# Layers 0, 1 and 3: the first block of the feed-forward part multiplies the input before its norm is known

## The reference, cut to what matters

```python
mod = (c_act @ ada_w[l] + ada_b[l])[:, None, :]
sh1, sc1, g1, sh2, sc2, g2 = jnp.split(mod, N_MOD, axis=-1)
...
x = x + g1 * token_mix(h, ...)
h = rmsnorm(x, norm2_g[l]) * (1.0 + sc2) + sh2
x = x + g2 * conv_ffn(h, ffn_up[l], conv_w[l], conv_b[l], ffn_down[l])

def conv_ffn(h, w_up, conv_w, conv_b, w_down):       # layers 0 and 1
    u = h @ w_up
    up = jnp.pad(u, ((0, 0), (pad, pad), (0, 0)))
    u = sum(up[:, i:i + S] * conv_w[i] for i in range(CONV_WIDTH)) + conv_b
    a, b = jnp.split(u, 2, axis=-1)
    return (jax.nn.gelu(a, approximate=False) * b) @ w_down

def sq_relu_mlp(h, w1, w2):                          # layers 2 and 3
    return jnp.square(jax.nn.relu(h @ w1)) @ w2
```

## Time and profile before

| | |
|---|---|
| median of 3 runs | 2072.24 us (2068.34 to 2072.96) |
| the profiled execution, its own time | 2072.03 us |
| its span, first to last instruction | 2070.3 us |
| PE busy | 2037.2 us, 98% |
| DVE busy | 1514.8 us, 73% |
| ACT busy | 987.7 us, 48% |
| POOL busy | 389.5 us, 19% |
| mean granted clock of TensorE | 0.994 of full speed |
| DMA | 396.38 MB, mean 191 GB/s |

### The profile page before, as it was taken

The page is one execution under the profiler, slowest core; times in us unless marked ns, Lnnn a source line. Parts: engine busy times, 40 slices in busy tenths (PEclk is TensorE's granted clock), DMA queues, the critical chain, the costliest instruction groups (busy, mean ns, idle before and its releaser), DMA issues.

```text
span 2070.3 us, 37115 instructions
## 1 busy us (share of the span) xinstructions
PE 2037.2 (98%) x14314; PEld 1872.9 (90%) x14314; DVE 1514.8 (73%) x2169; ACT 987.7 (48%) x1500; POOL 389.5 (19%) x284
## 2 busy tenths in 40 slices
PE   9999999999999999999999999999999999999998
PEld 8999999999999999999877888988888998899998
DVE  7877889977767999978988524898433285876554
ACT  4544456645445465553245533442143254755453
POOL 0421203300601213224101002120020021121120
PEclk9999999999999999999999999999999999999999
DMA  9775767786566656673554322366633244665553
GB/s 329 293 258 198 252 228 253 239 300 223 206 238 220 214 193 217 202 241 125 185 171 143 112 83 98 115 200 224 195 110 102 72 164 143 234 211 173 195 193 105
DMA packets 109739, 396.38 MB, mean 191 GB/s; under 512 B 12424, under 2 KB 13072, under 8 KB 109328
## 3 DMA queue, kind: packets, MB, share of 16 engines
q1 hardware_dynamic: 108304, 389.99, 55.7%
q0 software_dynamic: 1280, 4.20, 0.7%
HBM read 393.08 MB, written 1.05 MB: 190 GB/s over the span
## 4 chain that ended last, share of the span: by engine, by line
PE 79%; DVE 15%; DMA 2%; issue 2%; ACT 1%; POOL 0%; SPq 0%; DVEq 0%; ACTq 0%; POOLq 0%
PE bank L510 19%; PE bank L511 19%; PE bank L512 19%; DVE w_lo L1499 7%; DVE stage L1520 3%; DMA stage<-in_stream 2%; PE bank L708 2%; PE bank L635 2%; PE bank L634 2%; PE bank L633 2%; PE bank L711 2%; DVE conv L1790 1%; DVE conv L1795 1%; DVE rstd L1517 1%; PE bank L534 1%
## 5 line engine op out<-in xcount | busy, mean ns | idle before, releaser
L1499 DVE TENSOR_TENSOR w_lo<-stage,w_hi 128x1024 fp32r<-128x1024 f32 x536 | 716.7, 1352 | 411.0 <-ACT w_hi L1068 409.5
L1068 ACT ACTIVATE w_hi<-stage 128x1024 fp32r<-128x1024 f32 x536 | 566.3, 1060 | 840.3 <-PE bank L512 503.8
L510 PE MATMUL bank<-h_hi,w_hi 128*128 128x256 f32 (+1 forms) x2368 | 721.6, 305 | 8.6 <-DVE w_lo L1499 8.1
L511 PE MATMUL bank<-h_lo,w_hi 128*128 128x256 f32 (+1 forms) x2368 | 716.6, 303 | 0.0
L512 PE MATMUL bank<-h_hi,w_lo 128*128 128x256 f32 (+1 forms) x2368 | 716.4, 303 | 0.0
L510 PEld LDWEIGHTS bank<-h_hi,w_hi 128*128 128x128 f32 x2368 | 445.4, 188 | 37.4 <-DVE w_lo L1499 11.0
L512 PEld LDWEIGHTS bank<-h_hi,w_lo 128*128 128x128 f32 x2368 | 445.3, 188 | 21.5
L511 PEld LDWEIGHTS bank<-h_lo,w_hi 128*128 128x128 f32 x2368 | 445.5, 188 | 21.0
L1520 DVE SCALAR_TENSOR_TENSOR stage<-stage,cvec 128x1024 f32<-128x1024 f32 x192 | 259.9, 1355 | 12.5 <-DMA cols<-in_cols 9.2
L510 PE MATMUL bank<-f_hi,w_hi 128*128 128x256 f32 (+1 forms) x448 | 145.3, 324 | 0.0
L511 PE MATMUL bank<-f_lo,w_hi 128*128 128x256 f32 (+1 forms) x448 | 145.3, 324 | 0.0
(11 more groups left out here) (268 smaller groups left out, 3525.3 us busy)
## 6 DMA issues: line engine op xcount, KB each, us to landing
stage<-in_stream SPq DMA_DIRECT2D x728, 512.0 KB, 4.4
bias<-in_bias POOLq DMA_DIRECT2D x16, 256.0 KB, 3.4
cvec<-in_cvec SPq DMA_DIRECT2D x3, 512.0 KB, 5.1
X<-in_x SPq DMA_DIRECT2D x2, 512.0 KB, 6.1
decay<-in_decay SPq DMA_DIRECT2D x1, 1024.0 KB, 5.5
X<-in_x SPq DMA_DIRECT2D x1, 1024.0 KB, 8.5
out<-X SPq DMA_DIRECT2D x4, 256.0 KB, 2.1
rope<-in_rope SPq DMA_DIRECT2D x2, 256.0 KB, 4.7
```

The costliest lines, as they stand in the source:

```text
L510: mm(out, w_hi[:, slot, w], xh[:, c, 0:T], start=first, stop=False)
L511: mm(out, w_hi[:, slot, w], xl[:, c, 0:T], start=False, stop=False)
L1068: A(w_hi[:, m % NR, :], stage[:, n % NS, :], ACT.Copy).then_inc(hi_ready, 1)
L1499: do(V.tensor_tensor(w_lo[:, m % NR, :], stage[:, n % NS, :], w_hi[:, m % NR, :].bitcast(F32), ALU.subtract), unit_done, done_value(n))
```

## The change

For layers 0, 1 and 3:

- Block up0 (f0) multiplies raw_hi and raw_lo, the split of X*MUL without the norm. Each has two more columns, S and S+1, that hold the shift sh2, so a bank's column S is sh2 @ W. The products have 258 columns instead of 256. ScalarE makes raw_hi (raw_highs) and VectorE raw_lo (raw_lows), in two halves of 4 chunks behind the residual.
- TensorE makes the norm's sums before the third unit of up0 instead of before its first. The fill products and the chunkwise first unit are gone there. The blocks from up1 (f1) on use h as before.
- When rstd is there, VectorE copies column S (shifted) and multiplies each bank of up0 by rstd into tt (scale_first); ScalarE adds the shift in tt. The convolution (or relu) of block 0 then works on tt.
- The places of the weight splits move: three copies stand between ScalarE's squares and its root, and four splits on VectorE before the reciprocal. Block 0's elementwise work comes after up1's splits.
- In SCHEDULE the modulation of layer 1 starts at up2 instead of up0; for layer 2 it is every 3 units instead of 4 from ar1, and every 7 instead of 6 from up3.
- The first vector of layer 2's modulation for j < 4 takes one pass of 1024 with a scratch tile of its own (products).

```diff
-    (0, "k0", 0, 2, [(0, j) for j in range(4, 12)]), (0, "up0", 1, 3, [(1, j) for j in range(4)]),
-    (0, "dn0", 4, 1, [(1, 4), (1, 5)]), (1, "in", 5, 2, [(1, j) for j in range(6, 12)]),
-    (1, "ar1", 0, 4, [(2, 0), (2, 1)]), (1, "up3", 0, 6, [(2, 2)]), (1, "dn0", 0, 3, [(2, 3)]),
+    (0, "k0", 0, 2, [(0, j) for j in range(4, 12)]), (0, "up2", 0, 3, [(1, 0), (1, 1), (1, 2)]),
+    (0, "dn0", 2, 2, [(1, 3)]), (0, "dn0", 10, 1, [(1, 4), (1, 5)]), (1, "in", 5, 2, [(1, j) for j in range(6, 12)]),
+    (1, "ar1", 0, 3, [(2, 0), (2, 1)]), (1, "up3", 0, 7, [(2, 2)]), (1, "dn0", 0, 3, [(2, 3)]),
...
-                norm_sums(L, "n2")
-                fill_gap(L, "up0", 16)
-                feature_block(L, "up0", hh, hl, S, h_ready(L, "n2"), after_norm=(L, "n2"))
+                feature_block(L, "up0", raw_hi[L], raw_lo[L], S + 2, raw_ready(L), before={2: lambda: norm_sums(L, "n2")})
                 for b in range(1, FC // 2):
-                    feature_block(L, f"up{b}", hh, hl, S, nothing)
+                    feature_block(L, f"up{b}", hh, hl, S, h_ready(L, "n2") if b == 1 else nothing)
...
+            def late_norm(layer, ready, n):
+
+                advance(n - 4)
+                root_table(layer, "n2")
+                raw_highs(layer, ready, range(DC // 2))
+                advance(1)
+                squares(layer, "n2", ready, range(DC // 2), table=False)
+                advance(1)
+                raw_highs(layer, ready, range(DC // 2, DC))
+                advance(1)
+                squares(layer, "n2", ready, range(DC // 2, DC))
+                advance(3)
+                root(layer, "n2")
+                highs(layer, "n2", behind=(3,))
+
+            def shift_scaled(layer, g, n):
+
+                wait_taken(act, g)
+                A(tt[:, n, S:T2], tt[:, n, S:T2], ACT.Identity, bias=shifted[:, n:n + 1]).then_inc(s["scaled_ready"], 1)
+                act.wait_ge(s["scaled_ready"], 4 * layer + n + 1)
...
-                if vecs == 2:
+                if layer == 2 and j < 4:
+                    settle()
+                    do(V.scalar_tensor_tensor(products[:, :], w, 1.0, cvec[:, 0, :], ALU.mult, ALU.mult,
+                                              accum_out=MOD[:, par, 0, q:q + 1]))
+                elif vecs == 2:
...
+            def late_norm(layer):
+
+                advance(3)
+                norm(layer, "n2", behind=(4,))
+
+            def scale_first(layer, name):
+
+                for n in range(4):
+                    g = grp(layer, name, n)
+                    wait_filled(dve, g)
+                    do(V.tensor_scalar(shifted[:, n:n + 1], bank_of(g)[:, S:S + 1], 1.0, None, ALU.mult))
+                    settle()
+                    take(V.tensor_tensor(tt[:, n, S:T2], bank_of(g)[:, 0:S], rstd[:, 0:S], ALU.mult), g)
...
-                    ahead = 2 if nb == 0 else -2
+                    ahead = 1 if nb == 0 else -1
...
-                norm(L, "n2")
-                advance(1)
+                late_norm(L)
                 for b in range(FC // 2):
-                    g0 = most_of(L, f"up{b}")
+                    if b:
+                        g0 = most_of(L, f"up{b}", 2 if b == 1 else 0)
+                    else:
+                        advance(2)
+                        scale_first(L, "up0")
+                        advance(1)
```

More of the change, by code:

```diff
@@ L1038, in _ @@
                                         hooks={(0, 2, 0): lambda: norm_sums(2, "c2")})
-                        else:
-                            feature_block(L, f"f{b}", h_hi[L], h_lo[L], T, h_ready(L, "n2") if b == 0 else nothing,
-                                          after_norm=None if b else (L, "n2"))
+                        elif L == 3 and b == 0:
+                            feature_block(L, "f0", raw_hi[L], raw_lo[L], S + 2, raw_ready(L),
+                                          before={2: lambda: norm_sums(L, "n2")})
+                        else:
+                            feature_block(L, f"f{b}", h_hi[L], h_lo[L], T, h_ready(L, "n2") if (L, b) == (3, 1) else nothing)
                     base = 32 * (L - 2) + 16 * half
@@ L1090, in each, with root_table, squares @@
                     advance(1)
-            def squares(layer, name, ready, chunks):
+            def root_table(layer, name):
+                nth = NORMS.index((layer, name))
+                A(idle[0:1, nth:nth + 1], ones[0:1, 0:1], ACT.Sqrt).then_inc(s["idle"], 1)
+            def squares(layer, name, ready, chunks, table=True):
                 nth = NORMS.index((layer, name))
                 tok = tokens_of(name)
-                if 0 in chunks:
-                    A(idle[0:1, nth:nth + 1], ones[0:1, 0:1], ACT.Sqrt).then_inc(s["idle"], 1)
+                if 0 in chunks and table:
+                    root_table(layer, name)
                 for c in chunks:
@@ L1136, in norm, with raw_highs @@
                     highs(layer, name)
+            def raw_highs(layer, ready, chunks):
+                if 0 in chunks:
+                    ready(0)
+                    A(raw_hi[layer][:, :, S:S + 2], MOD[:, layer % 2, 0, 3 * DC:4 * DC].rearrange("p (c t) -> p c t", t=1).to_broadcast([P, DC, 2]),
+                      ACT.Copy).then_inc(s["raw_hi"], 1)
+                for c in chunks:
+                    ready(c)
+                    A(raw_hi[layer][:, c, 0:S], X[:, 0, c, :], ACT.Copy,
+                      scale=MUL[:, layer % 2, 0, 1, c:c + 1]).then_inc(s["raw_hi"], 1)
+            def late_norm(layer, ready, n):
[15 more added lines that the diff above has]
+                act.wait_ge(s["scaled_ready"], 4 * layer + n + 1)
             def first_norm(ready):
@@ L1443, in _ @@
                     for b in range(4 * half, 4 * half + 4):
-                        for part in range(2):
+                        late = L == 3 and b == 0
+                        if late:
+                            advance(2)
+                        else:
+                            for part in range(2):
+                                if (L, b) != (3, 1):
+                                    advance(1)
+                                if b % 4:
+                                    hidden2_hi(b - 1, part)
                             advance(1)
-                            if b % 4:
-                                hidden2_hi(b - 1, part)
-                        advance(1)
                         for n in range(4):
@@ L1606, in norm, with raw_lows @@
                 rest(layer, name, DC - 1)
+            def raw_lows(layer, chunks):
+                base = RAW_BEFORE[layer]
+                if 0 in chunks:
+                    dve.wait_ge(s["raw_hi"], base + 1)
+                    do(V.tensor_tensor(raw_lo[layer][:, :, S:S + 2],
+                                       MOD[:, layer % 2, 0, 3 * DC:4 * DC].rearrange("p (c t) -> p c t", t=1).to_broadcast([P, DC, 2]),
+                                       raw_hi[layer][:, :, S:S + 2].bitcast(F32), ALU.subtract), s["raw_lo"], base + 1)
+                for c in chunks:
+                    dve.wait_ge(s["raw_hi"], base + c + 2)
+                    do(V.scalar_tensor_tensor(raw_lo[layer][:, c, 0:S], X[:, 0, c, :], MUL[:, layer % 2, 0, 1, c:c + 1],
+                                              raw_hi[layer][:, c, 0:S].bitcast(F32), ALU.mult, ALU.subtract),
+                       s["raw_lo"], base + c + 2)
+            def late_norm(layer):
[8 more added lines that the diff above has]
+                    take(V.tensor_tensor(tt[:, n, S:T2], bank_of(g)[:, 0:S], rstd[:, 0:S], ALU.mult), g)
             def final_norm(layer):
@@ L1675, in residual @@
                                                 X[:, 0, c, :], ALU.mult, ALU.add), g0 + n)
+                if layer != 2 and name[:2] == "wo":
+                    settle()
+                    raw_lows(layer, range(4 * nb, 4 * nb + 4))
                 if before_norm:
```

92 lines of the change are left out of this document (68 added, 24 removed).

## The result

The change makes the kernel slower: 2076.44 us median of 20 runs against 2071.63 of 20 runs of before, a ratio of 1.0024 (+5.0 us), 95% interval 1.0016 to 1.0031, or +3.3 to +6.4 us. One run of before took 2725.8 us and is not in the ratio, which compares the fast runs of both kernels. The forecast was 2068.5, -3.5 us against its base. The side was wrong; the time lies in the stated range and near rival B.

A forecast was written before the change was run, and what follows sets the result against it. TensorE, busy 98%, was taken as the bound, with VectorE's weight splits feeding it. Terms +1.4 - 2.4 - 2.0 - 2.5 = -5.5 us, plus 2 for disturbances, gave -3.5 from 2072.0: 2068.5 us, range 2059 to 2078.

The forecast's parts named there:

- rival B: Slower: VectorE backlog at up2 in layers 0 and 1, GpSimd collisions, half clock, no modulation gain; +5, 2077 us; chance 0.22.
- the modulation's -2.5: Layer 2's modulation made in layer 1, with one pass and new spread: -2.5 us, bounds -5 to +3.
- Steps 1 and 3: Layer 0 from the output block to the norm's sums: ScalarE and VectorE feed in time, sums end at 287.5 without stall.
- Step 2: Start of up0: TensorE begins at once at 279.75 and runs units 0 and 1 to 285.2 free of a stall.
- the sign that its mechanism is wrong: New TensorE waits inside up0 itself would show the forecast wrong in its mechanism; no size given.
- Step 4: Up1 in layer 0: three weight copies delay the root, so TensorE stalls 2.1 us, then 0.5 us.
- Steps 5 and 6: Up2 in layer 0: late splits stall TensorE 2.6 us at the third unit, 3.7 at the fourth; up2 ends at 324.0.
- Layer 0's +1.4: Layer 0: 10.2 us of gap replaced by 2.2 of sums and 9.4 of stalls, +1.4 us.
- Layer 1's -2.4: Layer 1: stalls of 2.0, 0.4, 2.0 and 2.6 us, up3 at 42.6 instead of effectively 45.0 after the output product: -2.4 us.
- Layer 3's -2.0: Layer 3: stalls of 1.6 and 0.4 us at f1, which ends 25.9 instead of 27.9 us after the output product: -2.0 us.
- Disturbances, +2: Layers 0 and 1: splits meeting GpSimd products and half clock after waits add 2 us together, between nothing and 5.6.
- Two columns more: First-block products of 258 columns instead of 256 on 3 x 96 products: 0.25 us.

The follow-up runs named there:

- e1: The kernel before with the late norm in layer 3 only, SCHEDULE and two-pass modulation as before: ratio 0.9986, -2.9 us against before.
- e3: The kernel before with only the one pass of 1024 in place of two of 512, SCHEDULE as before: ratio 0.9955, -9.3 us against before.
- e7: The kernel before with the one pass and the late norm in layer 3 only, SCHEDULE as before: ratio 0.9970, -6.2 us against before.
- e8: The kernel before with the new SCHEDULE, the one pass and the late norm in layer 0 alone: ratio 1.0019, +3.9 us against before.
- e2: The kernel before with the modulation part alone (new SCHEDULE and one pass), all three norms as before: ratio 0.9996, -0.8 us against before.
- e11: The kernel before with one pass, late norm in layer 3 only, layer 1's modulation from up2, layer 2's spacing as before: ratio 0.9964, -7.5 us against before.
- e4: The change in full, but with SCHEDULE as before: ratio 1.0042, +8.7 us against before.
- e6: The change with GpSimd's product for blocks 0 and 1 of layers 0 and 1 cut to 16 of 256 columns: 1.0019, +3.9 us against before.
- e9: The change with layer 1's first twelve modulation blocks from up4 on instead of up2: ratio 1.0010, +2.1 us against before.
- e12: The change with no modulation block between the last output products and up4 in layers 0 and 1: ratio 1.0019, +3.9 us against before.
- e5: The change with up2's third-unit copy and split moved ahead of gelu and block 0's convolution steps, layers 0 and 1: 1.0069, +14.3 us against before.
- e10: New SCHEDULE, one pass and old norms, plus twelve unread VectorE steps in each of layers 0 and 1: ratio 1.0040, +8.3 us against before.

## Why the forecast was wrong, by its steps

The steps that failed are layer 1's (forecast -2.4 us, measured +6.1) and the modulation's -2.5. Between them they had two things wrong: a modulation block ahead of a residual was priced at nothing, and the denser blocks of the new SCHEDULE were taken as a gain on the whole, where they lose 4.0 us before the norm of layer 1. Below them lies an assumption: VectorE's waits were followed step by step from one trace, as if the rest of the layer were unchanged.

- **Steps 1 and 3** held: the sums come without a stall, 7.9 us behind W (forecast 7.75). **Step 2** held in layers 0 and 3 and failed in layer 1. There the residual stands behind a modulation block for two vectors, which I had seen and priced at nothing here, and up0's fourth group waits for it, 1.4 us in the list of waits above. The forecast had called new waits in up0 the sign that its mechanism is wrong; in layer 1 that sign is there. VectorE's timeline: the block is 738.33 to 741.55, the residual follows a split.

```profile
738.33 1.54 DVE L1585 SCALAR_TENSOR_TENSOR products<-stage,cvec 128x1024 f32<-128x1024 f32 x1
739.80 1.75 DVE L1595 SCALAR_TENSOR_TENSOR stage<-stage,cvec 128x1024 f32<-128x1024 f32 x1
742.09 1.21 DVE L1570 TENSOR_TENSOR w_lo<-stage,w_hi 128x1024 fp32r<-128x1024 f32 x1
743.41 1.66 DVE L1777 SCALAR_TENSOR_TENSOR X<-bank,MOD,X 128x256 f32<-128x256 f32 x4
```

- **Step 4**: forecast 2.1 and 0.5 us in up1, measured 0.2 and 0.3 (0.9 and 0.4 in layer 1, 0.2 in layer 3), below the 1 to 3 us that it named as a sign for all three layers. The root and the reciprocal come 1 us earlier than I had them: it ended at 290.73, W + 11.6, not W + 12.5, and up0's units take 2.9 to 3.0 us instead of 2.7.
- **Steps 5 and 6** were right in kind and nearly in size: 2.5 us (2.6) and 2.9 us (3.7), the latter with 1.6 us of half clock behind it. Up3 starts at W + 44.3; the forecast had 324.0 - 279.75 = W + 44.25.
- **Layer 0's +1.4** was right for that pair of traces: from W to up3 the change takes 1.1 us more. Its working has two slips. The stalls of steps 4 to 6 add up to 8.9, not 9.4, and 322.62 is the start of up2's third last product; up3 began at 322.96, W + 43.2. With either put right it is about +1. It failed in its base and in its end. I compared with one profiled execution of before. Other traces of the same code in layer 0 have W + 41.9 (e1), 41.7 (e3) and 39.1 (e7), because the gap itself varies from 5.8 to 9.9 us. And I stopped at up3: from there to layer 1 the change loses 2.1 us more, and 0.9 before W. With the same SCHEDULE the late norm in layer 0 costs 4.8 us (e8 less e2).
- **Layer 1's -2.4** failed most: up3 at W + 46.1, not 42.6, 2.4 us later than in the trace of before. The other 4.0 us are lost before W and belong to the modulation. Besides step 2, the block ahead of up3 takes 4.5 us (780.53 to 785.03), because each of its two passes meets a GpSimd instruction. TensorE waits 2.85 us there, where I had 0.8, and runs at half clock behind it.

```profile
780.53 2.33 DVE L1585 SCALAR_TENSOR_TENSOR products<-stage,cvec 128x1024 f32<-128x1024 f32 x1
782.80 2.30 DVE L1595 SCALAR_TENSOR_TENSOR stage<-stage,cvec 128x1024 f32<-128x1024 f32 x1
785.03 3.48 DVE L1570 TENSOR_TENSOR w_lo<-stage,w_hi 128x1024 fp32r<-128x1024 f32 x3
```

- **Layer 3's -2.0** held: -2.8 in the trace, -2.9 alone (e1). The surplus is the stall of 1.6 us at f1, which is 0.2.
- **The modulation's -2.5**: -0.8 with the old norms (e2). I had counted TensorE's waits that go against new ones of 0.8 to 1.4 us; e2's trace has one of 2.9 with half clock behind it, and loses 3.4 us in layer 1 up to W, the change's 4.0. By the runs the parts are -9.3 and +8.5, sizes that e7 and e11 put in doubt. With the late norms the new SCHEDULE helps instead (from e4 to the change, -3.7).
- **VectorE's split** was read as 536 times 1.22 us. The earlier trace rows has a mean of 1.35: 70 us over the kernel in which splits last longer than 1.22, which the forecast then counted only at two places.
- **Disturbances, +2**: half clock once in layer 0's stretch and twice in layer 1, once of it before W. One of them, the granted clock half in nearly all of a window behind the wait of 2.87 us:

```profile
318.60:322.10 3.50, 2.83 (x13) 0.51 0.75 214
```

- **Two columns more** were priced at 0.25 us. A product of 128x258 starts 0.121 us after the one before it, one of 128x256 0.113 to 0.115: 288 of them cost about 2 us.

Rival B named the right place and nearly the right sum, partly by luck: of its parts the GpSimd collisions at up2 are small (e6), half clock follows only some of the stalls, a stall at up3's last unit isn't there (layer 1 has one at up3's first), and the 4.0 us before layer 1's norm are in none of them. By ratios, late norms in layers 0 and 1 cost 5.0 + 2.9 + 0.8 = 8.7 us (the change, less layer 3's gain, less e2), for 11 us of VectorE. From W to up3 it is 3.2 and 3.7 us, the change against e2, and there the cause is shown: TensorE waits for a chain of VectorE's own work plus 4.6 to 4.8 us of waits for ScalarE (e9, e12). Why the rest is lost, behind up3, stays open. In the gap VectorE did the norm's work while TensorE ran fill products; the late norm puts that work, and 5.5 us more, beside products that need VectorE's splits.

## What to carry to other kernels

Before filling a gap of the busiest engine, write down what the second engine does in the gap and where that work will stand afterwards, with the waits that the new order gives it. Here the gap was filled, and the same time came back as waits further on, because the second engine's chain had become the longer one. Its length is work plus waits: moving one copy and one split cost 9.3 us with no work added (e5), and taking 2.8 us of work out of the stretch made it 2.8 us shorter (e9). Don't read an engine's busy share as its load where its steps can be held up by another engine: the same 121 steps took 91.5 us in one trace and 78.8 in another (e2, e10). Take the base from several executions where a gap varies between them, and test the parts of a joined edit alone: the part with the one pass gains by itself, in a change that loses.

## What was unexpected

- One pass of 1024 for two of 512 gave 9.3 us for 5.6 us less work. About 5 of the 8 us between the traces are in layer 1; 1.4 is a spell of half clock near 1046 us in layer 2, where neither kernel differs, which is shorter in e3. The rest is not accounted for.
- Some stretches have a product every 0.118 us instead of 0.113 at a granted clock of 1.00, in other layers in other executions (layer 0 of e10 from up3 to dn0, layer 3 of e9): 0.1 us a unit, 3.4 us in that stretch of e10. Why wasn't tried.
- Whether the 258-column product is slower for its columns or for where raw_hi and raw_lo lie (rows of 384) wasn't tried either.
